# Tokens gathered for eight experts at a time, and six items of expert weights fetched before the expert stage

## The reference

```
x = x + memory_cross_attention(rms_norm(x, norm_mem_w[l]), rms_norm(mem, norm_memkv_w[l]), ..., w_mo[l])
x = x + hierarchical_moe(rms_norm(x, norm_moe_w[l]), w_group[l], w_router[l], w_exp_gate[l], w_exp_up[l], w_exp_down[l])
...
grp = jnp.argmax(g_logits, axis=-1)
top_vals, top_idx = lax.top_k(e_logits, EXPERT_TOP_K)
expert_id = grp[:, None] * EXPERTS_PER_GROUP + top_idx
...
xb = t_pad[toks]
return (jax.nn.silu(xb @ w1[e]) * (xb @ w3[e])) @ w2[e]
...
y = jax.ops.segment_sum(y_slots * slot_gate[:, None], slot_tok, num_segments=N + 1)[:N]
```

## Time and profile before

| | |
|---|---|
| median of 3 runs | 2017.01 us (2015.54 to 2018.52) |
| the profiled execution | 2016.81 us, span 2015.0 us |
| expert stage | from 1483.9 us to the end |
| first expert product | 1520.67 us |
| end of the last `contract` | 2002.82 us |
| PE busy over the span | 1887.5 us (94%) |
| DVE, ACT, POOL busy | 803.5, 663.2, 542.4 us |
| expert weights | 192 DMAs of 1 MB, medians 9.0 to 10.5 us from issue to landing |

### The profile page before, as it was taken

One profiled execution on the slowest core, in us unless ns is written; L12 is line 12 of the kernel. 1 busy time (PEld: TensorE's weight loads), 2 busy tenths in 40 slices (PEclk: granted clock), 3 DMA queues, 4 the chain that ended last, 5 costly groups with the idle time before them and its releaser, 6 DMA issues. The chain is left out here.

```text
span 2015.0 us, 28970 instructions
## 1 busy us (share of the span) xinstructions
PE 1887.5 (94%) x11709; PEld 1389.1 (69%) x11709; DVE 803.5 (40%) x1639; ACT 663.2 (33%) x1380; POOL 542.4 (27%) x420
## 2 busy tenths in 40 slices
PE   6999989998999989999999998999979999999997
PEld 4788977878788666677787876988765444444443
DVE  4467462254332355532524146143242343343333
ACT  4542233222224344446245246444332111111110
POOL 2342233225553333248145321253300000000000
PEclk9999999999899989899999999999989999999999
DMA  5230122123123212143132221232157999999994
GB/s 159 63 88 24 43 73 63 42 63 122 36 63 106 63 33 63 32 164 97 50 123 84 85 97 40 65 105 84 43 215 315 419 411 414 419 418 419 420 419 178
DMA packets 133209, 313.40 MB, mean 156 GB/s; under 512 B 15296, under 2 KB 103120, under 8 KB 108496
## 3 DMA queue, kind: packets, MB, share of 16 engines
q1 hardware_dynamic: 133072, 311.49, 41.5%
HBM read 309.37 MB, written 2.10 MB: 155 GB/s over the span
## 5 line engine op out<-in xcount | busy, mean ns | idle before, releaser
L321 POOL TENSOR_TENSOR unit_low<-unit_ring,unit_high 128x512 fp32r<-128x512 f32 x332 | 436.5, 1340 | 796.1 <-ACT unit_high L314 796.1
L358 PE MATMUL dense<-hT,unit_high 128*128 128x512 f32 x592 | 243.8, 412 | 3.0 <-DVE dense_temps L528 1.7
L359 PE MATMUL dense<-hT,unit_high 128*128 128x512 f32 x592 | 234.1, 395 | 0.0
L360 PE MATMUL dense<-hT,unit_low 128*128 128x512 f32 x592 | 233.9, 395 | 0.0
L314 ACT CAST unit_high<-unit_ring 128x512 fp32r<-128x512 f32 x332 | 185.9, 619 | 57.3 <-PE dense L360 28.2
L451 PE MATMUL dense<-unit_high,hT 128*128 128x256 f32 x704 | 203.7, 289 | 0.7 <-POOL unit_low L321 0.4
L452 PE MATMUL dense<-unit_low,hT 128*128 128x256 f32 x704 | 199.7, 284 | 0.0
L453 PE MATMUL dense<-unit_high,hT 128*128 128x256 f32 x704 | 199.7, 284 | 0.0
L451 PEld LDWEIGHTS dense<-unit_high,hT 128*128 128x128 f32 x704 | 135.5, 193 | 8.0 <-issue 2.6
L452 PEld LDWEIGHTS dense<-unit_low,hT 128*128 128x128 f32 x704 | 135.5, 192 | 0.6 <-issue 0.5
L453 PEld LDWEIGHTS dense<-unit_high,hT 128*128 128x128 f32 x704 | 135.4, 192 | 0.0
(11 more groups left out here) (590 smaller groups left out, 3472.5 us busy)
## 6 DMA issues: line engine op xcount, KB each, us to landing
expert_ring<-w_exp_gate SPq DMA_DIRECT2D x64, 1024.0 KB, 9.6
expert_ring<-w_exp_up SPq DMA_DIRECT2D x64, 1024.0 KB, 10.5
expert_ring<-w_exp_down SPq DMA_DIRECT2D x64, 1024.0 KB, 9.0
unit_ring<-w_in SPq DMA_DIRECT2D x55, 1024.0 KB, 5.3
unit_ring<-w_br SPq DMA_DIRECT2D x16, 512.0 KB, 6.4
unit_ring<-w_mkv SPq DMA_DIRECT2D x8, 1024.0 KB, 5.4
x<-x SPq DMA_DIRECT2D x8, 512.0 KB, 5.7
w_out_raw<-w_out SPq DMA_DIRECT2D x4, 1024.0 KB, 10.2
```

Of the source, the lines that this page charges most:

```text
L321: nc.gpsimd.tensor_tensor(low[:, at:at + 512], raw[:, at:at + 512], high[:, at:at + 512], ALU.subtract).then_inc(*self.split.up())
L358: nc.tensor.matmul(out, high[:, k, c], rh, start=(k == 0), stop=False)
L359: nc.tensor.matmul(out, high[:, k, c], rl, start=False, stop=False)
L360: last = nc.tensor.matmul(out, low[:, k, c], rh, start=False, stop=(k == kd - 1))
```

## The change

`GROUP` goes from 256 to 512 columns, that is eight experts, so there are four groups of four pairs in place of eight of two. Each group has eight gather jobs of 8 products with 512 columns; they all stand in the group's last pair (`q == 3`): two behind `expand`, two behind `turn_hidden`, two between the two `contract` steps and two behind them. The other pairs carry none. `xT` is no longer double buffered. `pick_tokens` fills the 512 columns in two halves. `pick_tokens` for the next group runs, as before, at the group's first pair. At the head, the rest of the rows 2 and 3 moves from DVE to GpSimd, as a scaling (`scale_xn`) and a subtraction (`rest_of_scaled`).

The ring of expert items is laid over the memory of `block_two`, and SP issues items 0 to 5 there, each behind a wait for the data that lay in its slot. Some small tiles are placed in other tiles' space.

```diff
 N_OVER = -(-((2 * SEQ - N_EXPERTS) // SLOTS) // 2) * 2
 N_BLOCKS = N_EXPERTS + N_OVER
 N_CMP = 31
-GROUP = 256
+GROUP, HALF_GROUP = 512, 256
 PAIR = 2 * SLOTS
 
...
+    @section.sync
+    def _(sp):
+
+
+        for n, token in enumerate((values_done, S.mem_scored, S.mem_scored, S.mem_jobs_turned, S.mem_mixed[3], S.mem_mixed[3])):
+            sp.wait_ge(*token)
+            experts.load(sp, n)
     run(dense_residual(core, ring, S, "mem_o", x, [S.chunk["turned", k] for k in range(KD)]))
 
 
...
+    order = [("gather", 0, k) for k in range(KD)]
     for p in range(N_EXPERTS // 2):
-        g, q = p // 2, p % 2
+        g, q = p // 4, p % 4
         if p == 0:
             order += [("spread", 0, i) for i in range(4)]
         else:
             order += [("scatter", p - 1, i) for i in range(2 * NT)]
-        if g + 1 < N_EXPERTS // 4:
-            order += [("gather", g + 1, 2 * q), ("gather", g + 1, 2 * q + 1)]
+        if q == 3 and g + 1 < N_EXPERTS // 8:
+            order += [("gather", g + 1, k) for k in range(KD)]
         if 1 <= p <= 3:
...
 
 
     def load_items(sp):
-        for n in range(ITEMS):
+        for n in range(len(experts.token), ITEMS):
             if n >= RING:
                 sp.wait_ge(*used.at(n - RING + 1))
-            dst, src = item(n)
-            for e in range(2):
-                sp.dma_start(dst[:, e], src[:, e]).then_inc(*landed[n % RING].up(16))
+            experts.load(sp, n)
 
 
     def turn_x(pe):
...
         nc.tensor.matmul(side[2][:, 3 * E:NT * E], ones_r, both_r[:, 0:E], start=False, stop=True).then_inc(*ranked.up())
 
-    def gather(pe, g, i):
-        job = ("gather", g, i)
+    def gather(pe, g, k):
+        job = ("gather", g, k)
         pe_wait_side(pe, job)
-        bank = side_bank(job)
-        for half in range(2):
-            chunk = slice((2 * i + half) * P, (2 * i + half + 1) * P)
-            out = bank[:, half * GROUP:(half + 1) * GROUP]
-            for t in range(NT):
-                if i == 0 and half == 0:
-                    if g == 0:
-                        pe.wait_ge(*xn_rest.at(t + 1))
-                    pe.wait_ge(*token_pick.at(NT * g + t + 1))
-                nc.tensor.matmul(out, xn_hi[:, t, chunk], pick[:, t, :], start=(t == 0), stop=False)
-                last = nc.tensor.matmul(out, xn_lo[:, t, chunk], pick[:, t, :], start=False, stop=(t == NT - 1))
+        bank, chunk = side_bank(job), slice(k * P, (k + 1) * P)
+        for t in range(NT):
+            if k == 0:
+                if g == 0:
+                    pe.wait_ge(*(xn_rest.at(t + 1) if t < 2 else xn_pool_rest.at(t - 1)))
+                pe.wait_ge(*token_pick.at(2 * NT * g + 2 * t + 2))
+            nc.tensor.matmul(bank[:], xn_hi[:, t, chunk], pick[:, t, :], start=(t == 0), stop=False)
+            last = nc.tensor.matmul(bank[:], xn_lo[:, t, chunk], pick[:, t, :], start=False, stop=(t == NT - 1))
         last.then_inc(*filled.up())
 
     def spread(pe, i):
@@ -3795,20 +3832,21 @@
         last.then_inc(*filled.up())
 
     def expand(pe, p, i):
-        n, g, q = 6 * p + i, p // 2, p % 2
+        n, g, q = 6 * p + i, p // 4, p % 4
         bank = gate_bank if i < 2 else up_bank
+        if i < 2:
+            wait_read(pe, ("gather", g, 4 * i + 3))
         if i == 0:
-            wait_read(pe, ("gather", g, 3))
             if p:
                 pe.wait_ge(*silu_s.at(p))
         if i == 2 and p:
             pe.wait_ge(*gated.at(p))
-        pe.wait_ge(*landed[n % RING].at(32 * (n // RING + 1)))
+        pe.wait_ge(*experts.token[n])
         view, _ = item(n)
         for k in range(4):
             for e in range(2):
                 s = slice(q * PAIR + e * S, q * PAIR + (e + 1) * S)
-                last = nc.tensor.matmul(bank[e * S:(e + 1) * S, :], xT[:, g % 2, 4 * (i % 2) + k, s], view[:, e, k, :],
+                last = nc.tensor.matmul(bank[e * S:(e + 1) * S, :], xT[:, 4 * (i % 2) + k, s], view[:, e, k, :],
                                         start=(i % 2 == 0 and k == 0), stop=(i % 2 == 1 and k == 3))
         last.then_inc(*used.up())
 
...
 
-    def keep_tokens(act, g, i):
-        job = ("gather", g, i)
-        if i == 0:
-
-            act.wait_ge(*(used.at(6 * (2 * g - 3) + 4) if g >= 2 else logits_s.at(1)))
+    def keep_tokens(act, g, k):
+        job = ("gather", g, k)
+        if k == 0:
+
+            act.wait_ge(*(used.at(6 * (4 * g - 1) + 4) if g else logits_s.at(1)))
         wait_filled(act, job)
-        for half in range(2):
-            k = 2 * i + half
-            last = nc.scalar.mul(xT[:, g % 2, k, :], side_bank(job)[:, half * GROUP:(half + 1) * GROUP], part_gain[:, k:k + 1])
-        last.then_inc(*side_a.up())
+        nc.scalar.mul(xT[:, k, :], side_bank(job)[:], part_gain[:, k:k + 1]).then_inc(*side_a.up())
 
...
                                        op0=ALU.mult, op1=ALU.subtract).then_inc(*xn_rest.up())
+
+    def scale_xn(pool, t):
+        if t == 2:
+            pool.wait_ge(*inverted.at(1))
+            pool.wait_ge(*squared.at(2))
+        nc.gpsimd.tensor_tensor(scaled[t - 2], x[:, t, :], rs[:, t:t + 1].to_broadcast([P, D]), ALU.mult).then_inc(*xn_scaled.up())
+
+    def rest_of_scaled(pool, t):
+        pool.wait_ge(*xn_scaled.at(t - 1))
+        pool.wait_ge(*xn_rounded.at(t + 1))
+        nc.gpsimd.tensor_tensor(by_part(xn_lo[:, t, :]), scaled[t - 2].rearrange("p (m k) -> p k m", k=KD), by_part(xn_hi[:, t, :]),
+                                ALU.subtract).then_inc(*xn_pool_rest.up())
...
     def pick_tokens(dve, link, g):
-        src = slots
+
         if g:
-            link(nc.vector.tensor_scalar(rel[:], slots[:], float(GROUP * g), None, ALU.subtract))
-            wait_filled(dve, ("gather", g - 1, 3))
-            src = rel
+            wait_filled(dve, ("gather", g - 1, KD - 1))
+        first = slots
+        if g:
+            nc.vector.tensor_scalar(rel[:, 0], slots[:], float(GROUP * g), None, ALU.subtract)
+            first = rel[:, 0]
+        link(nc.vector.tensor_scalar(rel[:, 1], slots[:], float(GROUP * g + HALF_GROUP), None, ALU.subtract))
+        halves = [(first, slice(0, HALF_GROUP)), (rel[:, 1], slice(HALF_GROUP, GROUP))]
         for t in range(NT):
-            last = nc.vector.tensor_scalar(pick[:, t, :], iota[:, 0:GROUP], src[:, 0, t:t + 1], None, ALU.is_equal)
+            for src, cols in halves:
+                last = nc.vector.tensor_scalar(pick[:, t, cols], iota[:], src[:, 0, t:t + 1], None, ALU.is_equal)
         link(last)
         for t in range(NT):
-            nc.vector.scalar_tensor_tensor(out=pick[:, t, :], in0=iota[:, 0:GROUP], scalar=src[:, 1, t:t + 1],
-                                           in1=pick[:, t, :], op0=ALU.is_equal, op1=ALU.add).then_inc(*token_pick.up())
+            for src, cols in halves:
+                nc.vector.scalar_tensor_tensor(out=pick[:, t, cols], in0=iota[:], scalar=src[:, 1, t:t + 1],
+                                               in1=pick[:, t, cols], op0=ALU.is_equal, op1=ALU.add).then_inc(*token_pick.up())
 
     def gate_tokens(dve, link):
         dve.wait_ge(*exped.at(1))
...
                             scatter(pe, p - 1, s)
-                if g + 1 < GROUPS:
-                    gather(pe, g + 1, 2 * q)
+                for k in itertools.islice(tokens, 2):
+                    gather(pe, g + 1, k)
                 turn_hidden(pe, p)
-                if g + 1 < GROUPS:
-                    gather(pe, g + 1, 2 * q + 1)
+                for k in itertools.islice(tokens, 2):
+                    gather(pe, g + 1, k)
                 contract(pe, p, 0)
+                for k in itertools.islice(tokens, 2):
+                    gather(pe, g + 1, k)
                 contract(pe, p, 1)
+                for k in tokens:
+                    gather(pe, g + 1, k)
                 if 1 <= p <= 3:
                     account_sums(pe, p)
             for s in range(2 * NT):
@@ -4207,6 +4269,13 @@
                     with pe.If(n_over > 2 * o):
                         spill_products(pe, o)
                 pe.wait_ge(*spilled.at(1))
+
+        @block.gpsimd
+        def _(pool):
+            scale_xn(pool, 2)
+            scale_xn(pool, 3)
+            rest_of_scaled(pool, 2)
+            rest_of_scaled(pool, 3)
 
         @block.scalar
         def _(act):
...
```

More of the change, by code:

```diff
@@ L2685, in blocks @@
         output_projection(core, ring, S, x, xin, merged, post_gain, w_high, lambda k: w_low[:, k, :], temps, turn_memory, mem_keys)
-        block_two(core, ring, S, x, place, load, temps, mem_keys, memT, kT_mem, route, route_landed)
+        block_two(core, ring, S, x, place, load, temps, mem_keys, memT, kT_mem, route, route_landed, experts)
     st.close()
+    return experts
 def wait_for(engine, tokens):
@@ L3447, in memory_channels, with block_two @@
     S.mem_mixed[h] = mixed
-def block_two(core, ring, S, x, place, load, temps, mem_keys, memT, kT_mem, route, route_landed):
```

(51 more changed lines are left out.)

88 lines of the change are left out of this document (44 added, 44 removed).

## The result

| | median us | range | runs |
|---|---|---|---|
| before | 2016.28 | 2008.58 to 2018.52 | 4 |
| changed | 2042.71 | 2037.06 to 2049.23 | 4 |

The changed kernel is slower. The medians differ by 26.4 us, and 2041 was forecast. The ratio on record, 1.0144 with a 95% interval of 1.0121 to 1.0167, stands for +29.0 us (+24.4 to +33.7). Its profiled execution took 2039.71 us, with a span of 2037.4 against 2015.0 before.

What follows compares the result with a forecast made beforehand. PE's own queue, in the order written, was taken to set pairs 1 to 13. The terms -21.7 + 34.2 + 6.0 + 3.0 + 4.1 - 1.0 = +24.6 us on 2016.8 gave 2041 us, range 2030 to 2048.

Steps and rivals of the forecast that it cites:

- pairs without gather: Ten pairs losing their gather jobs: 4.04 us of work leaves each, only 2.17 is gained; -21.7 us in all.
- pairs with it: Pairs 3, 7, 11 taking all of a group's gather jobs: +11.4 us each, +34.2 in all.
- picks at pairs 4, 8, with the cold clock: Wider pick on DVE delays add_rows, PE stands 3.0 us: +6.0 us; slow clock behind the stands: +3.0.
- pair 0: First pair of the expert stage: -2.0 us for the second gather job, +1.0 for cold clock on contract; -1.0.
- head: Expert stage up to the first expand: rests, wider picks and wider first gather sum to +4.1 us (1 to 6).
- early items: Six expert items issued in block_two: cost nothing and gain nothing, since PE did not wait for an item.
- Lost cover: Between last expand and contract: without gather jobs PE waits for hidden and actT, so only 2.17 of 4.04 us is gained.
- Wide products: Gather products of 512 columns: 0.232 us each like scatter products, 64 products taking 14.85 us.
- The rival at 0.12: A 512-column gather product takes no more than a 256-column one, 0.12 us: 2014 us, chance 0.03.
- The weights: Expert weight transfers don't bind the pairs; the rival that they bind pairs without gather gave 2060 us, chance 0.06.
- GpSimd's part: In the head, GpSimd's rests are hidden if done by about 1507; without that cover up to 2 us.
- -4.1 for the rests: In the head, DVE's last two rests no longer delay the choice of experts: -4.1 us.

Runs made afterwards that it cites:

- late pick: Changed kernel with pick_tokens for the next group moved behind gate_hidden on DVE; 2034.27 us, stage 552.8 us.
- no early items: Changed kernel with no expert item fetched in block_two, all seven issued at the stage's start; 2045.65 us, stage 561.8 us.
- version with pairs of 26.5 us: Changed kernel with three scatter jobs kept as cover behind the last expand and the transposes in pairs without gather jobs; 2026.15 us, ratio to before 1.0074.
- version with cover and late pick: Changed kernel with scatter jobs as cover, next group's tokens picked behind hidden, and rests of rows 2 and 3 on DVE; 2015.64 us, ratio 1.0023.
- the rests on DVE: Changed kernel with the rests of rows 2 and 3 back on DVE, GpSimd idle in the stage; 2043.08 us, stage 561.2 us.
- the subtractions in halves: Changed kernel with each GpSimd subtraction of 1024 columns made as two of 512; 2036.41 us, stage 561.55 us.
- before once more: The kernel before, unedited, profiled again; 2015.14 us, ratio 1.0009, stage 532.2 us.

## Why the prediction was right, and its miss in the head

The prediction had the sign and the size: 2041 for 2042.71. That the two lie 1.7 us apart is partly luck: the stage grew by 5.7 us more than the sum, and the blocks ahead of it happened to end 7.9 us earlier in the profiled execution. Against the trace, step by step:

| step | forecast us | measured us | from |
|---|---|---|---|
| pairs without gather | -2.17 each | -2.2 (pairs 1, 2, 6) | chain |
| pairs with it | +11.4 each | +11.4 (pair 11) | chain |
| picks at pairs 4, 8, with the cold clock | 4.5 each | 4.3 and 4.5 | late pick |
| from pair 1 on, sum | +21.5 | +21.4 | 481.5 - 460.1 |
| pair 0 | -1.0 | -0.2 | 34.07 - 34.26 |
| head | +4.1 | +9.1 | first expand |
| early items | 0 | 0 | no early items |
| stage | +24.6 | +30.3 | |

Pairs 1 and 2 take 28.2 and 28.5 us and not the 27.9 that the prediction named, since `account` jobs stand in them, as in before (30.4 and 30.7); the difference is the same.

- **Lost cover** was the step that mattered, and it is now shown from both sides. Taking the cover from before costs 2.4 to 3.3 us a pair with the same work; giving the changed kernel another cover wins 1.36 a pair.
- **Wide products**: the gather products follow each other by 0.23 us, the rate of the scatter products. The rival at 0.12 is out.
- **The weights** bound neither the changed kernel nor a version with pairs of 26.5 us. The prediction argued it from pair 14 and from the pair with gather jobs that gives the lead back. Both hold: from 1540 us on, landings took 17.4 us at most in the changed kernel and 20.9 in its version with cover and late pick.
- **The step that failed** is GpSimd's part, costed at nothing ("GpSimd's part is hidden if it is done by about 1507"; "Without that cover it costs up to 2 us"). It asked only when GpSimd would be done, and not what DVE does meanwhile. GpSimd was done at 1494.68, well in time, and it was DVE that lost: 2.10 + 2.77 - 0.34 = 4.5 us, on the path that sets the first gather. Of the -4.1 for the rests 3.7 came true. These two, 4.5 + 0.4, are the miss of 5.0. From `hidden` to the first `expand` the head grew by 12.7 us, of which 4.5 are the lock; the 8.2 that are left are the sum's 1.8 + 7.3 - 0.9 = 8.2.
- **That this 8.2 fits is in part luck.** By the kernels with the rests on DVE the gather and the picks cost 7.1 us, and moving the rests 2.0 where -4.1 was forecast. The sum is the same, +9.1, but the 1.1 us between 7.1 and 8.2 go with the clock: the gather began 5.8 us before its return to 1.00 here, 3.2 us before it with the rests on DVE, and 4.8 in before. The prediction kept these 4.8 although its own sum started the gather 2.3 us earlier.
- **Pair 0**: PE's stand grew to 4.3 us; `contract` took 9.30 us in place of 7.78, +1.5 where the prediction had +1.0, and the transposes 1.14 in place of 0.75, for which it had nothing. These two are about the 0.8 between -1.0 and -0.2.

The medians differ by 26.4 us and the stages by 30.3. The interval of the ratio, +24.4 to +33.7 us, holds both. The head has two forms, in which the change costs +9.1 and +7.4 us, and the blocks ahead of the stage differ by several us from run to run; which forms stand in the runs without a trace isn't known. So the runs' times can't tell the sum's 24.6 from the stage's 30.3, and only the traces show the miss.

## What to carry to other kernels

Work that stands between two dependent steps also hides the wait between them: before taking it away, read in a place without it what it covered, since only the difference is gained (2.17 of 4.04 us here), and then look for other work that could stand there. When work moves to an idle engine, ask which operations of the busy one it can hold up, here those with two inputs in SBUF, and not only whether the idle engine ends in time. And read a head or a tail in several traces before a term of one us is taken from it: here the changed kernel had its first `expand` 45.8 or 46.4 us after the start, and the one before 36.7 or 39.0.

## What the runs showed of the hardware

- A DVE instruction with two inputs in SBUF that meets a GpSimd instruction stands until that one ends, up to 2.1 and 2.8 us here for 0.17 us of work; a reduction with one input (0.16) and an operation with one of its two inputs in PSUM (0.29) don't. The rest of row 0, 2.67 us in place of 2.11, lies beside GpSimd's scaling. It works the other way too: in the four traces with whole subtractions and the second form of the head, GpSimd's first subtraction began beside DVE's rest of row 1 and took 3.38 to 3.42 us in place of 2.86.
- In the head an earlier start of the gather products isn't a gain of the same size, since part of them runs before the granted clock is back at 1.00. In before they began 25.8 us after the stage's start and the clock rose in the 31st us; in the changed kernel they began at 28.3 and it rose in the 35th; with the subtractions in halves they began at 27.9 and it rose in the 35th all the same. With the rests on DVE they began at 27.5 and it rose in the 31st. Why it rose later with GpSimd at work in the changed kernel isn't shown.
- The clock of the blocks ahead of the stage differs from run to run. The changed kernel and before once more, from 200 to 300 us, where both run the same code:

```profile
200.00:300.00 100.00, 88.09 (x733) 81.30 (x730) 58.11 (x90) 32.25 (x62) 31.40 (x22) 1.00 0.22 65
```

```profile
200.00:300.00 100.00, 90.55 (x695) 83.63 (x691) 53.41 (x82) 31.89 (x62) 29.33 (x21) 0.95 0.20 58
```

  At a clock of 1.00 PE got through 733 instructions in place of 695. In the thirteen traces the stage starts between 1472.6 and 1484.3 us, and so a span alone says little of a change of a few us; the stage does. The starts aren't spread evenly: 1480.1 to 1484.3 in the five traces of kernels made from before, 1472.6 to 1481.6 in the eight made from the changed one, 5.4 us earlier in the mean. Why is open; the time ahead of the stage may thus hide part of the stage's +30.3 in the medians.
